# Head sums and their spreading as quarter products, with a new order of the recurrence's work

## The reference, cut to what matters

```
kk = heads(k * k_k)
kk = kk / jnp.maximum(jnp.sqrt(jnp.sum(kk * kk, axis=-1, keepdims=True)), 1e-12)
k = k * (1.0 + (a - 1.0) * k_a)
...
mean = jnp.mean(out, axis=-1, keepdims=True)
var = jnp.mean(jnp.square(out - mean), axis=-1, keepdims=True)
out = ((out - mean) * lax.rsqrt(var + LNX_EPS)).reshape(B, T, D) * lnx_w + lnx_b
bonus = jnp.sum(r_h * k_h * r_k, axis=-1, keepdims=True) * v_h
```

## Time and profile before

| what | value |
|---|---|
| median of three runs | 3540.37 us |
| profiled execution | 3546.33 us, its span 3544.6 us |
| recurrence, first to last product | 411.8 to 1126 us of the span |
| TensorE busy over the span | 3381.6 us (95%) |
| VectorE, ScalarE, GpSimd busy | 1652.6, 1354.5, 1740.5 us |

### The profile page before, as it was taken

The page is one execution under the profiler, slowest core; times in us unless marked ns, Lnnn a source line. Parts: engine busy times, 40 slices in busy tenths (PEclk is TensorE's granted clock), DMA queues, the critical chain, the costliest instruction groups (busy, mean ns, idle before and its releaser), DMA issues. The chain is left out here.

```text
span 3544.6 us, 87445 instructions
## 1 busy us (share of the span) xinstructions
PE 3381.6 (95%) x33525; PEld 2940.6 (83%) x33525; DVE 1652.6 (47%) x3032; ACT 1354.5 (38%) x2917; POOL 1740.5 (49%) x1622
## 2 busy tenths in 40 slices
PE   8999889998898999999999999999989999999999
PEld 8999778777777998888888887777769988888887
DVE  7113356555554374444444533333343744444444
ACT  6212445554443133333333434444453333333335
POOL 4434266666654445454554544344433354545455
PEclk9999899999999999999999999999999999999999
DMA  4422211111114011111111234444442111111111
GB/s 154 154 88 89 71 35 36 43 41 38 38 44 143 10 45 46 48 44 45 44 46 47 87 85 96 114 102 91 107 108 66 41 46 47 43 50 42 47 44 73
DMA packets 432743, 233.86 MB, mean 66 GB/s; under 512 B 190979, under 2 KB 417043, under 8 KB 431558
## 3 DMA queue, kind: packets, MB, share of 16 engines
q1 hardware_dynamic: 428882, 215.40, 21.9%
q10 hardware_dynamic: 3572, 14.33, 1.0%
HBM read 187.69 MB, written 47.21 MB: 66 GB/s over the span
## 5 line engine op out<-in xcount | busy, mean ns | idle before, releaser
L2688 DVE TENSOR_TENSOR H<-ps,H 128x512 f32<-128x512 f32 x608 | 419.6, 690 | 463.3 <-PE ps L2351 462.5
L2239 POOL TENSOR_TENSOR split<-work,split 128x512 fp32r<-128x512 f32 x280 | 379.8, 1361 | 493.9 <-ACT split L2510 486.8
L2351 PE MATMUL ps<-split,split 128*128 128x512 f32 x1824 | 514.0, 390 | 0.0
L2404 PE MATMUL ps<-xs,split 128*128 128x512 f32 x1920 | 512.5, 393 | 0.0
L1341 PE MATMUL ps<-arena 64*64 64x64 f32 (+1 forms) x9984 | 400.9, 225 | 37.9 <-issue 21.2
L1341 PEld LDWEIGHTS ps<-arena 64*64 64x64 f32 x9984 | 351.6, 135 | 71.4 <-issue 45.6
L2404 PEld LDWEIGHTS ps<-xs,split 128*128 128x128 f32 x1920 | 349.9, 188 | 68.2
L2351 PEld LDWEIGHTS ps<-split,split 128*128 128x128 f32 x1824 | 339.8, 188 | 70.9 <-DVE H L2688 0.7
L2404 PE MATMUL ps<-split,split 128*128 128x512 f32 x1440 | 366.1, 390 | 0.5 <-issue 0.5
L3278 PE MATMUL ps<-xs,split 128*128 128x384 f32 x1656 | 361.4, 355 | 2.6 <-POOL split L3192 2.6
L601 PE MATMUL ps<-mixed,wsplit_mix 128*128 128x384 f32 x1872 | 331.7, 339 | 7.6 <-DVE mixed L824 7.6
(11 more groups left out here) (325 smaller groups left out, 5972.4 us busy)
## 6 DMA issues: line engine op xcount, KB each, us to landing
work<-in_ffn_w_gu SPq DMA_DIRECT2D x168, 256.0 KB, 2.9
work<-in_ffn_w_down SPq DMA_DIRECT2D x168, 128.0 KB, 2.3
work<-in_cache_v SPq DMA_DIRECT2D x64, 256.0 KB, 3.9
work<-in_cache_k SPq DMA_DIRECT2D x256, 64.0 KB, 2.2
rkv_scratch<-lora ACTq DMA_DIRECT2D x24, 576.0 KB, 2.8
stage_mix<-in_rwkv_w_rkv SPq DMA_DIRECT2D x24, 512.0 KB, 3.8
work<-in_attn_w_qkv SPq DMA_DIRECT2D x24, 512.0 KB, 4.2
h_scratch<-H SPq DMA_DIRECT2D x2, 4608.0 KB, 12.5
```

The source lines that it names most:

```text
L2239: pool.tensor_tensor(w[1], frm, w[0].bitcast(F32), ALU.subtract).then_inc(u_lo, 1)
L2351: last = pe.matmul(full(DOWN + j % 2), w[part][:, (m % 2) * P:(m % 2 + 1) * P], mem.hid[xpart][:, SEG[h]], start=(a == 0), stop=(a == 2))
L2404: last = pe.matmul(full(to), unit(i)[part][:, k * P:(k + 1) * P], operand[xpart][:, k, :], start=(first and k == 0 and a == 0), stop=(k == ...
L2688: dve.tensor_tensor(at, full(DOWN + j % 2), at, ALU.add).then_inc(added, 1)
```

## The change

`sums` and `expanded` no longer use the whole array. Both work by thirds with `cross`: six blocks of 64 frames per third, each two quarter products. The sums take 16 moving columns of ones; the spreading multiplies by a 64 by 64 identity. `ksum` and `vsum` become three items each. `joined` gets a new merge, `under`: the first half of an inversion level, or a `fold`, with one third of a norm, the products alternating.

The squared keys are written to the buffer of r times k (`rkr`) and no longer to that of `k2`; `kq` waits for `bonus_done` alone, and `rkr` waits for the sums instead of `k2`. In a pair's preparation the key sums come first, then the three `a` products and `k2`, then `w` and the scans, the spreading, `b`, the decays and the writes. The order is new: START spells out pair 0 whole, PATTERN the seven others.

```diff
-SUM_COLS = 56
-FIRST = (
-    "CCCCCCCCCCCCCCCCCCCCBBBCCCBCCCCBCCEBECBBEBCBCECFFBCFCCFCCFEBFCFCEBCCFCCCBEBEBFCECCFECFECCCE")
+START = (
+    "CCCCCCCCCCCCCCCCCCCCCCCBBBACBCCCEBCBEFBBECCFFCCECFCCEBEBFCECFECCCCCBFCEBBCECECFCEFBFCACAFBBFAEACECAEACAEFAFCAF"
+    "AEAFCAAECACCBFBECFAACECEFCAECECFAEECBAAEFBCAFEBBEACABECBFAEBCACBEFCCAECAFCAACFCAEFBCBAECAFAAABEACFEAECBFAEACCA"
+    "CEBFBEAFAABEBAEACAFAECFAFCCE")
 PATTERN = (
-    "EBADFBAEDABEAFDFEADAFBAEFAAECDADADBFECAFEACFBEBCFAEDAECCAABFAEADAECAFCEADABFCEABECACFAEACEAAEFCAFCAEECABABFAAA"
-    "EFACBEACAFBECCAACFACEBBFCAAEAFCEBBECAAEFCEAFEACFCCE")
+    "DADAFAEDEAFADBEDFABEDAFBEBFACEDABFADEAAAEFDBEACBAECFBAACEFACADEECFBACEAFCCEBABEACFACEAFACCADAEAEACFCECAFCCBFEA"
+    "DEACFBECFBAECBFAAEBFEAEBAAFECAACCACAEBAFAAAECFAECFCACEC")
...
-    out = [("kq", o, None)]
+    out = [("kq", o, None)] + [("ksum", o, c) for c in range(3)] + [("a", o, c) for c in range(3)] + [("k2", o, None)]
     for c in range(3):
-        out += [("w", o, c), ("a", o, c), ("scan", o, c)]
-    out += [("ksum", o, None)] + [("decays", o, c) for c in range(3)]
-    out += [("kexp", o, c) for c in range(3)] + [("k2", o, None), ("b", o, None)] + [("write", o, g) for g in range(NG)]
+        out += [("w", o, c), ("scan", o, c)]
+    out += [("kexp", o, c) for c in range(3)] + [("b", o, None)] + [("decays", o, c) for c in range(3)] + [("write", o, g) for g in range(NG)]
     return out + [("rkr", o, None)] + [("rk", o, c) for c in range(3)]
...
+NORMS = ("ksum", "kexp", "vsum", "affine")
...
+        elif before and before[0] in NORMS and (key[0] == "fold" or key[0] == "invert" and key[2][2] == 0):
+            out[-1] = ("under", key[1], (key, before))
+        elif before and key[0] in NORMS and (before[0] == "fold" or before[0] == "invert" and before[2][2] == 0):
+            out[-1] = ("under", before[1], (before, key))
...
-LAST_BANKS = {("center", 0): 4, ("center", 1): 5, ("ns", 1): 4, ("nst", 0): 5, ("affine", 1): 5, ("affine", 2): 4,
+LAST_BANKS = {("center", 0): 4, ("center", 1): 5, ("ns", 1): 4, ("nst", 0): 5, ("vsum", 1): 4, ("vsum", 2): 5, ("affine", 1): 5, ("affine", 2): 4,
...
-                    pool.wait_ge(kinv, pr + 1)
...
                     pool.wait_ge(k2_ready, pr + 1)
+                    pool.wait_ge(kinv, pr + 1)
                     pool.tensor_tensor(m.rkr, m.r, m.k2, ALU.mult).then_inc(rk_ready, 1)
...
-            def sums(out, squares):
-                for i in range(T // P):
-                    last = pe.matmul(out[:, SUM_COLS * i:SUM_COLS * (i + 1)], squares[:, i * P:(i + 1) * P],
-                                     mem.headones[:, 64 - SUM_COLS // 2:64 + SUM_COLS // 2], start=True, stop=True)
-            def expanded(out, roots, c):
-                for i in range(3):
-                    last = pe.transpose(out[:, i * P:(i + 1) * P], roots[:, (3 * c + i) * P:(3 * c + i + 1) * P], mem.ident[:, :])
+            def sums(pb, squares, c, j):
+                return cross(pb[:, TS * j:TS * j + TS], squares[:, c * CW + 64 * j:c * CW + 64 * j + 64], mem.ones[:, 0:TS])
+            def expanded(pb, roots, c, j):
+                return cross(pb[:, 64 * j:64 * j + 64], roots[:, c * CW + 64 * j:c * CW + 64 * j + 64], None)
...
-            STREAMED = {("w", 0): 30, ("w", 1): 4, ("w", 2): 4, ("a", 0): 4, ("a", 1): 4, ("a", 2): 4, ("ksum", None): 4,
+            STREAMED = {("w", 0): 30, ("w", 1): 4, ("w", 2): 4, ("a", 0): 4, ("a", 1): 4, ("a", 2): 4, ("ksum", 0): 4,
...
+                elif what == "under":
+                    (turn, _, inner), (norm, np, c) = arg
+                    g = inner if turn == "fold" else inner[0]
+                    G = GROUPS[g][1]
...
+                    norm_start(norm, np, c)
+                    for q in range(G):
+                        last = fold_part(g, q) if turn == "fold" else square(pr, g, inner[1], q)
+                        for j in range(6 * q // G, 6 * (q + 1) // G):
+                            norm_part(norm, np, c, j)
+                    last.then_inc(folded[LINE[g]] if turn == "fold" else m1_done[LINE[g]], 1)
...
                 elif what == "kq":
                     act.wait_ge(k_in, 16 * pr + 16)
                     if pr:
-                        act.wait_ge(written_pool, NG * pr)
-                        act.wait_ge(rk_ready, pr)
-                    act.activation(m.k2, m.k, ACT.Square, scale=vp("kk", pr)).then_inc(kq_ready, 1)
-                    if pr:
                         act.wait_ge(bonus_done, pr)
+                    act.activation(m.rkr, m.k, ACT.Square, scale=vp("kk", pr)).then_inc(kq_ready, 1)
```

More of the change, by code:

```diff
@@ L1035, in recurrence_order @@
     out = []
-    for letter in FIRST:
+    rest["A"] = serial_items(0)
+    for letter in START:
         out.append(rest[letter].pop(0))
-    for o in range(PAIRS):
-        threads = {"A": serial_items(o) if o + 1 < PAIRS else last_serial_items(), "D": finish_items(o - 1) if o else []}
+    assert not rest.pop("A")
+    for o in range(1, PAIRS):
+        threads = {"A": serial_items(o) if o + 1 < PAIRS else last_serial_items(), "D": finish_items(o - 1)}
         for letter, n in per_pair.items():
@@ L1060, in recurrence_order @@
     for_tensor = list(out)
-    for c, after in enumerate((("vsum", o, None), ("affine", o, 2), ("nst", o, 0))):
+    for c, after in enumerate((("vsum", o, 2), ("affine", o, 2), ("nst", o, 0))):
         for_tensor.remove(("gate", o, c))
@@ L1463, in _ @@
                 e = pr % 2
-                if what in PIECES:
+                if what in PIECES and what not in ("ksum", "kexp", "vsum", "affine"):
                     b, n = PIECE_OF[key]
@@ L1474, in _ @@
                     last.then_inc(piece_done[b], 1)
-                elif what == "ksum":
-                    pe.wait_ge(kq_ready, pr + 1)
-                    sums(pb, m.k2).then_inc(piece_done[b], 1)
-                elif what == "kexp":
-                    pe.wait_ge(kroot, pr + 1)
-                    expanded(pb, m.kkn, arg).then_inc(piece_done[b], 1)
+                elif what in ("ksum", "kexp", "vsum", "affine"):
+                    norm_start(what, pr, arg)
+                    for j in range(6):
+                        norm_part(what, pr, arg, j)
                 elif what == "rk":
@@ L1490, in _ @@
                     cross(pb[:, 0:CW], m.center, third(m.out, arg)).then_inc(piece_done[b], 1)
-                elif what == "vsum":
-                    for c in range(3) if pr == PAIRS - 1 else (2,):
-                        cb, cn = PIECE_OF["center", pr, c]
-                        pe.wait_ge(piece_free[cb], cn + 1)
-                    sums(pb, m.post1).then_inc(piece_done[b], 1)
-                elif what == "affine":
-                    pe.wait_ge(vroot, pr + 1)
-                    expanded(pb, m.post1, arg).then_inc(piece_done[b], 1)
                 elif what == "gate":
@@ L1691, in _ @@
                     act.copy(m.vb[:, e, c0:c0 + G, :], part(m.v)).then_inc(written_act, 1)
-                elif what == "ksum":
+                elif what == "ksum" and arg == 2:
                     if pr:
@@ L1697, in _ @@
                     act.activation(blocks(m.kkn), m.rs[:, 0, :].unsqueeze(2).to_broadcast((P, 18, 64)), ACT.Sqrt).then_inc(kroot, 1)
-                elif what == "vsum":
+                elif what == "vsum" and arg == 2:
                     act.wait_ge(vinv, pr + 1)
```

75 lines of the change are left out of this document (53 added, 22 removed).

## The result

The changed kernel took 3638.48 us (median of four runs, 3634.4 in the profiled one) against 3539.63 for the kernel before beside it: ratio 1.0274 (95%: 1.0253 to 1.0294), so it is 97 us slower. Forecast were 3524.8, and 3503 to 3547 as the range. (One of the four runs was disturbed and is left out of the ratio.)

The account below looks back on a forecast made before the run. TensorE's queue, busy 95%, was taken as the bound. Terms +1.0, -23.5, -3.4 and -1.5 gave -27.4 us; three quarters, -20.6, plus 5 for the opening made -15.6: 3524.8 us, range 3503 to 3547.

Parts of the forecast that it names:

- -3.4 and -1.5: TensorE's queue: us saved by nine more `both` items and by 32 `beside` items instead of 17.
- the opening: Pair 0's preparation: reordered chain makes the first form 6.8 us late, part of it regained; booked +5 us.
- What lies under other work: TensorE's queue: 52 `under` items, each priced at its longer part, hide 23.5 us of norm work.
- rival without concurrency (3): Mixed norms don't run side by side, so the 23.5 us don't come: queue -4, total 3542 us; chance 0.04.
- Norms, added: TensorE's queue: 96 new norm thirds take 68.0 us against 67.0 for the old sums and spreading, net +1.0.
- How much of it reaches the end: Whole kernel: between none and all of the 27.4 us queue saving arrives; three quarters taken, 20.6 us.
- rival (1): TensorE's idle pieces grow by nearly as much as its queue shortens, single-bank norm pieces included: 3539 us; chance 0.14.
- r and v late (2): At `write`, engines wait for the r and v transfers, loaded too late under the new order: 3547 us; chance 0.11.
- three table loads a pair: ScalarE: one of four table loads a pair goes for pairs 3 to 7, 1.28 us each.
- More than forecast (4): All 27.4 us arrive, 1 us of idle a pair also goes, the opening is regained: 3506 us; chance 0.13.

Follow-up runs that it names:

- whole_array_new_order: Changed kernel's order, buffers and thirds, but sums and spreading as whole-array products, nothing mixed with them: 3610.21 us, ratio 1.0191 to the kernel before.
- new_not_mixed: Changed kernel with the same products and order but no `under` items, a norm third's records before or behind the square's: 3637.13 us, ratio 1.0272.
- split_forms: Kernel before, with both 128-column products of every form cut into two of 64 columns, 1152 records more: 3560.04 us, ratio 1.0055.
- merge_forms: Kernel before, with identity columns behind each chunk of `ar`, merging one transposing product into its neighbour, 576 records fewer: 3531.88 us, ratio 0.9968.
- merge_both_products: Kernel before, with identities on either side of `ar`, so both form products also make the transposed copies, 1152 records fewer: 3524.48 us, ratio 0.9958.
- new_forms_merged: Changed kernel with both form products merged through identities on either side of `ar`, 2304 TensorE instructions fewer: 3618.64 us, ratio 1.0212.
- quarters_old_order: Changed kernel's quarter products and buffers with each norm item in its place in the order before, nothing mixed: 3573.57 us, ratio 1.0089.
- known_causes_k2_at_b: New order with whole-array norms, old opening, last writes moved later, both form products merged and `k2` right ahead of `b`: 3564.13 us, ratio 1.0058.
- new_old_opening: Changed kernel with pair 0's preparation in the old order: 3633.34 us, ratio 1.0254.

## Why the prediction was wrong, step by step

Three steps failed. Two runs split the miss. whole_array_new_order is the new order alone: the prediction's terms for it are three quarters of -3.4 and -1.5, and +5 for the opening, together +1, and it measured +67. The new products with their mixing were three quarters of +1.0 and -23.5, together -17, and measured +28.

**"What lies under other work", -23.5 us, measured 0.** The duration of a mixed item was right: an `under` item with 24 sums and 16 products of a level starts at 791.39, and the next item's first product comes at 792.07, so 40 records took 0.68 us, and 0.71 had been forecast.

```profile
791.39 0.19 PE L1356 MATMUL ps<-ones,arena 64*64 64x16 f32 x1
...
792.07 0.25 PE L1356 MATMUL ps<-arena 64*64 64x64 f32 x1
```

What failed first is the price without the mixing. I took it as the sum of the two parts, 1.18 us, and it is 0.88 (above), so that an item could save 0.16 us and not 0.47. Over the five middle pairs the busy time fell by 5.0 us, where 35 items at 0.47 would have been 16. What failed next is the step from one item to a pair. 40 records are 80 instructions in 0.68 us, 118 per us; the packets bring 256 in about 4 us, 64 per us. A stretch that mixes much uses up what is there and then stands still until the next packet: for 1.03 us until 793.46, 0.4 us of work behind this very item, and for 1.39 us some 250 instructions later (above). The mixed item of the earlier trace rows has the same rate, 112 instructions in 0.95 us, and could draw on what lay ready. An unmixed run, two instructions in 0.0295 us or 68 per us, takes them about as fast as they come. That overlap beyond it pays for a moment and not for a pair fits the 5.0 us of busy time saved and the 4.5 us of "issue" waits added. The rival without concurrency (3) had the price of this nearly right (-4 for the queue) by luck, since its reason was wrong: the products do run side by side, and even unmixed. I had read the row that pointed to it, 13.6 us "to no releaser" in the earlier trace rows, as too small to matter, and not asked what it was.

**"Norms, added", +1.0 net, measured +28 to +31.** Priced by the array's rate, 0.0295 us a record, the new sums and spreading cost the same as the old. TensorE's busy time bears that out where nothing is mixed: 3402.4 us in new_not_mixed and 3402.2 in whole_array_new_order. What the term left out is their number: 1872 records more, 3744 instructions, 15 packets (230 against 215). The doses, with the waits for "issue" in the five middle pairs:

| edit | packets | us | "issue" waits |
|---|---|---|---|
| split_forms | +9 | +20 | +7.7 |
| merge_forms | -4.5 | -11 | -5.7 |
| merge_both_products | -9 | -15 | -12.9 |
| new_forms_merged | -9 | -20 | -15.5 |
| norms on the new order | +15 | +28 | +29.4 |
| quarters_old_order | +15 | +31 | -5.9 |

A packet goes with 1.7 to 2.5 us; the intervals of the single edits allow 0.9 to 3.6. In the first five rows the waits at the packets' ends move with it, and for the four form edits, which change hardly anything else, the instructions are shown as the cause. (split_forms and merge_forms both have 6.8 us at the lower clock in the five pairs, so this doesn't explain their opposite signs.) That a packet costs about half of its 4 us, because TensorE waits for other things too, is argued and not shown. The last row has the same size without these waits: there the norms' waits for VectorE (7.1 us more in the five pairs) and the lower clock (up to 10) are seen instead, and how much the instructions cost is open. The first of these is what rival (1) named: single-bank pieces with a hop to VectorE each.

**"How much of it reaches the end", three quarters of a gain, measured a loss of 67 us.** I weighed only how much of the shorter queue would survive, between all and none, and took the order itself as neutral. No row of before could show the new order's waits, and so the bound should have gone below zero, as high as a hop to another engine at each moved item. This is the largest miss: the order's part was put at +1 us and measured 67. whole_array_new_order puts 17.5 us of its 65.7 in the trace before pair 1's first step, 39.7 in the five middle pairs (448.2 against 408.5) and 8.5 in the last two. Of the 67 the runs name 15 to 18 for the writes at the pair's start and 5 to 7 for the opening. With `k2` ahead of `b` some 5 more go (3610 less these two and some 18 for the merged forms would be 3569, and 3564 was measured), which is within the noise. The clock hangs on the first: in the changed kernel it is at its lower level of 1.2 GHz for some microseconds about once a pair, behind the idle piece at the first step. Granted clock is the third value from the end:

```profile
783.00:785.20 2.20, 0.00 (x0) 0.03 (x1) 2.06 (x5) 0.76 (x2) 1.51 (x2) 1.00 0.85 181
...
789.00:790.00 1.00, 1.00 (x21) 1.00 (x21) 0.23 (x1) 0.66 (x3) 1.00 (x1) 0.50 0.00 0
790.00:794.00 4.00, 2.97 (x136) 2.83 (x136) 1.51 (x5) 0.59 (x2) 4.00 (x5) 1.00 0.01 4
```

In the kernel before the middle pairs are at 1.00 throughout, and with the writes moved (600 to 1040 us) the mean is 0.99. From the opening to the phase's last product the lower level lasts 37.5 us in the kernel before and 75.1 in whole_array_new_order, so that up to 19 of the 67 us may be this (an estimate: half of the difference).

**What stays open.** About 35 us: known_causes_k2_at_b against merge_both_products. In the middle pairs TensorE's waits for VectorE are no larger than in merge_both_products (14.8 us for 16.8); those for ScalarE, with `center`'s copy (L1764) at 6.3, are the one kind that grew clearly. Most of the loss lies before: of the 54 us between the ends of the phase in the two traces, 29.7 come before pair 1's first step, and there the mean clock is 0.84 against 0.96. (The profiled run took 13 us more than the median of its four.) Pair 0's body also loses over 10 us that the old opening doesn't give back: in new_old_opening the first form is 3.6 us later than before and pair 1 15.6. The order START of pair 0 was not tried alone. No run added instructions without products either, so that a packet's price is a fit over edits and not a time that a row shows.

**The opening, +5, measured 5 to 7.** The first form came at 454.88, 9.7 later than before and not 6.8. The root and the sigmoids were as forecast in length. Off was the start of the sums: VectorE's first bound stood until a transfer of constants landed, and the three were done at 427.6 and not 423.8. The 30 streamed products took 5.12 us where I had 6.5.

```profile
423.97 0.16 DVE L1814 TENSOR_SCALAR arena<-ps 128x6 f32<-128x6 f32 x1 [13.35 <-DMA arena<-const_scratch]
...
427.44 0.17 DVE L1814 TENSOR_SCALAR arena<-ps 128x6 f32<-128x6 f32 x1 [1.57 <-PE ps L1356]
```

```profile
434.97 5.12 PE L1488 MATMUL ps<-ones 128*128 128x256 bf16 x30
```

The bounds lie 1.73 us apart, where 1.9 had been forecast for each sum: the hop through the single bank was priced right, and the wait for the constants was left out. The row with the transfer was there to be read, since in the kernel before VectorE's scans waited for the same transfer.

**r and v late (2): it didn't happen.** SyncE's and VectorE's rows, answering to the earlier trace rows:

```profile
752.67 14.88 SPq L1173 DMA_DIRECT2D arena<-rkv_scratch  x6
```

```profile
776.87 0.94 DVE L1835 SCALAR_TENSOR_TENSOR arena<-arena 128x252 f32<-128x252 f32 x1
```

The last transfer is issued by 767.6 and landed some 2.4 us later, near 770; `write` begins at 776.87 without idle time. 7 us were left, not 0 to 4: the longer pairs gave them back. The forecast of three table loads a pair held: in the five middle pairs ScalarE has three lines with five such loads each, where the kernel before has four. Each is 1.28 us, and TensorE's wait for ScalarE grew all the same, from 0.6 to 9.0 us in the five pairs.

**The other two.** That waits take it all (1) had the direction and not the size: it let them grow by as much as the queue shortens, and they grew by ten a pair beside a queue whose busy time grew by one. More than forecast (4) needed less idle time, and there is twice as much.

## What to carry to other kernels

Count TensorE's instructions beside its busy time: where small products run side by side, two records and two weight loads each, the time can be set by how fast instructions arrive, here 256 in about 4 us, and a product that does more columns at once is then worth more than one that overlaps. "Issue" waits inside an item whose inputs are ready, at multiples of 256 instructions, are the sign, and the instruction queue's packets on the page are the dose. Price an overlap against neighbours as they run now, not against the sum of their parts. A change of order gets a bound below zero like any other unknown: list for every engine what it is doing when a pair's first serial product needs it, before the queue's length is counted.

## What the runs showed of the hardware

TensorE's instructions come in packets of 16 KB for 256 instructions, about 4 us apart and never under 3.2 in the phase's middle pairs of any trace, even with nothing else in the queues (eight in 32 us, above). Quarter products of f32 ran at 118 instructions per us for one item and didn't hold it. Products of diagonal and off-diagonal quarters in neighbouring items overlap without alternating: 40 records in 0.88 us, for 1.18 at the rate of 0.0295 each. A mean share of 95% busy hid the waits for instructions, since a product's row lasts 0.22 us while the next is due in 0.03.
